# A hybrid layer's read-out in four groups of four tiles, and an output projection that turns x1 itself

## The chip, the cores and the metric

The kernel runs on one core of one Trainium2 chip. The metric is device time in microseconds (us), the median of several executions. Lower is better. All data is float32. A float32 product on TensorE is recorded as two matmul instructions, so "x2" in a row is one product.

## What is computed

One layer with a context prefix (256 tokens) and a latent stream (512 tokens), 1024 channels. What the change touches, cut from the reference:

```python
# per direction d of the recurrence: y is (tokens, heads, 64)
outs.append(group_norm(y, lnx_w, lnx_b) + bonus)          # mean and variance over the 64 of a head
rwkv_y = (outs[0] + outs[1]) * g                          # g = sigmoid(xg) @ g2
pool_y = (box_mean(u) - u) @ pool_w * pool_scale           # four windows: 2, 4, 8, 16
m = (sigmoid(gl_p) * (pool_y @ pool_proj) + sigmoid(gl_r) * (rwkv_y @ rwkv_proj)) @ w_out
h = x + gt1 * rmsnorm(m, norm_gains[1])                    # x1 below
u = rmsnorm(h, norm_gains[2]) * (1 + sc2) + sh2            # f below
logits = u @ [router_group_w, router_expert_w] + bias      # 36 columns
f = hier_moe(u, ...)                                       # top-1 of 4 groups, top-2 of 8 experts, 32 experts in all
out = h + gt2 * rmsnorm(f, norm_gains[3])
```

## The kernel before

The program is a row of blocks, one after another, each with its own instruction list for every engine and a barrier at its end: `begin`, `low_rank_inputs`, `prepare`, `recurrence` (until 836 us), `read_out`, `merge`, `project_out`, `route`, `experts`. The order in each list is written out by hand, and every cross-engine dependence is a wait for a semaphore. An engine runs its list in order, so a wait holds all that is behind it.

**read_out** (L997). The two directions' outputs are 16 tiles of 128 channels (two heads) x 512 tokens, `tile(d, k)`. For every tile TensorE makes the mean over a head (`ro_mean`, a product with a block matrix, L1060), VectorE subtracts it (L1112), ScalarE squares (L1091), TensorE makes the variance (`ro_var`, L1066), and ScalarE makes 1/root of it as `Ln` (L1099) and `Exp` with a scale of -0.5 (L1102), for two tiles at a time. The root is a full 128 x 512 tile: all 64 rows of a head hold the same numbers. VectorE multiplies (L1117), and for each k adds the two directions (L1122), applies gain and bias (L1124), adds `bonus` (L1126) and multiplies by the gate (L1129), which TensorE made at L1073. Between these lie eight pool steps (L1044 and L1048), alternately four products with a box matrix and one product with `pool_w`, through one PSUM bank that ScalarE reads (L1081, L1083). `y0`, the first direction, comes back from HBM by a transfer issued at the start (L1026). The tiles alternate between `ro_y` (direction 0) and `pool_space` (direction 1).

**merge** (L1138) is 224 products of 128 x 512 on TensorE, with the conditioning rows 2 to 5 of `mod_rows` worked out by VectorE beside them.

**project_out** (L1254). For each of four tiles of 128 tokens, `product` (16 products into `po_ps`, L1306); ScalarE's sum of squares (L1336) and root (L1339), VectorE's normalisation (L1367) and x1 = x + ... (L1369); sum of squares and root of x1 (L1341, L1344), VectorE's scale and shift to f (L1375, L1377), two 128 x 1024 steps; then TensorE turns f (`turn`, L1314), ScalarE copies it (`po_fT`, L1348), and `route` makes the 36 logits (L1322, L1323). TensorE's order is product(0), product(1), turn(0), route(0), product(2), turn(1), route(1), and so on. SyncE's queue loads rows, gains, x and the weights of three experts, then stores x1 and f of each tile, and the block ends when the stores of f have landed.

**route** (L1397) is a chain of small VectorE steps that sorts tokens to experts. SyncE loads the weights of three more experts meanwhile (L1437). It ends in gathers of token rows from f in HBM.

**experts** (L1607). 16 pairs of experts. Per pair: a gather of 128 rows, `turn` (L1644), `copy_xT` on ScalarE (L1653), gate and up products with 32-column tiles (L1794), sigmoid (L1656), two VectorE products (L1662, L1664), a turn, a copy, the down products (L1809), a copy of the result (L1659), a store. Weights live in seven slots. The transfer for expert n of 7 and up waits until the pair that last used its slot is through `down` (L1712). Each expert is 3 MB.

## Time and profile before

| | us |
|---|---|
| runs | 1563.69, 1564.85 (median), 1569.78 |
| profiled execution, its own time | 1565.51 |
| span of the profile | 1563.5 |
| mean granted TensorE clock | 0.939 of 2.4 GHz |
| busy: TensorE, VectorE, ScalarE | 1338.7 (86%), 634.8 (41%), 561.8 (36%) |
| read_out | 836 to 940 |
| merge | 940 to 1154 |
| project_out | 1154 to 1238.5 |
| route, to the first turn of experts | 1238.5 to 1270 |
| experts and the combination | 1270 to 1563.5 |

The time of an execution is 2 us above its span. Busy shares are means over stages that have different limits, so the table is only a map. What each stage waits for has to be read in the stage.

### The profile page before, as it was taken

The numbers are of one execution on the slowest core, as the hardware profiler recorded it, in microseconds if no ns is written. First come the engines' busy times: TensorE is split into PE (matmuls) and PEld (weight loads), VectorE is DVE, ScalarE is ACT, GpSimd is POOL, SyncE is SP. The second block draws the span as 40 slices with busy tenths as digits, with TensorE's granted clock in tenths as the row PEclk, the third lists the DMA queues.
The fourth block names the chain that finished last, engine by engine and source line by source line (L and its number), as shares of the span: only waits on it lengthen the run. The fifth ranks groups of instructions, "written<-read, shape, count | busy, mean of one in ns | idle before, by whom it ended". The sixth has DMA issues, their size and how long they took to land. (4 is left out here: it accounts for less than half of the span.)

```text
span 1563.5 us, 37612 instructions
## 1 busy us (share of the span) xinstructions
PE 1338.7 (86%) x16458; PEld 804.1 (51%) x16458; DVE 634.8 (41%) x982; ACT 561.8 (36%) x859; POOL 234.9 (15%) x191
## 2 busy tenths in 40 slices
PE   5889999999999999999997669899999559777780
PEld 2445555555888888888884224344434323222220
DVE  1357777773455544455442350533413330000004
ACT  4244454542655655565552560000002101111113
POOL 0011123112122433333310000000000011010002
PEclk9999999999999999999998889999999669998995
DMA  8205665546221222222205009644446369999985
GB/s 369 88 1 160 176 186 151 168 117 190 101 71 71 71 77 78 77 78 78 78 11 231 5 0 369 255 147 156 155 169 266 156 259 399 423 427 424 424 351 188
DMA packets 102761, 281.42 MB, mean 180 GB/s; under 512 B 18627, under 2 KB 67907, under 8 KB 88531
## 3 DMA queue, kind: packets, MB, share of 16 engines
q1 hardware_dynamic: 96660, 249.81, 43.0%
q0 software_dynamic: 5952, 29.36, 4.8%
q8 instruction: 126, 2.06, 0.5%
q14 instruction: 23, 0.19, 0.0%
HBM read 234.05 MB, written 53.49 MB: 184 GB/s over the span
## 5 line engine op out<-in xcount | busy, mean ns | idle before, releaser
L391 PE MATMUL pr_ps<-hT,pr_w 128*128 128x512 f32 x384 | 172.2, 602 | 4.0 <-DVEq L99 4.0
L972 DVE COPY_PREDICATED rc_T<-masks_sb,rc_ps 128x512 f32<-128x512 uint32 x96 | 65.2, 729 | 151.3 <-PE rc_ps L761 151.3
L391 PEld LDWEIGHTS pr_ps<-hT,pr_w 128*128 128x128 f32 x384 | 72.1, 191 | 94.9 <-issue 90.1
L1200 PE MATMUL mg_ps<-hT,mg_w 128*128 128x512 f32 x256 | 113.6, 602 | 3.2 <-PEq L1021 3.2
L1662 DVE TENSOR_TENSOR mg_w<-mg_w,ex_pgu 128x256 f32<-128x256 f32 x16 | 6.7, 422 | 192.4 <-ACT mg_w L1656 192.4
L1200 PEld LDWEIGHTS mg_ps<-hT,mg_w 128*128 128x128 f32 x256 | 49.5, 194 | 66.8 <-issue 66.8
L761 PE MATMUL rc_ps<-rc_T,rc_Z 64*64 64x64 f32 x3840 | 74.1, 221 | 6.8 <-issue 5.3
L1219 ACT ACTIVATE mg_sig<-mg_ps 128x512 f32<-128x512 f32 x16 | 9.6, 597 | 188.5 <-PE mg_ps L1200 188.5
L912 ACT ACTIVATE rc_G<-rc_ps 128x512 f32<-128x512 f32 x120 | 66.4, 599 | 24.0 <-PE rc_ps L761 23.3
L734 PE MATMUL rc_ps<-masks_sb,rc_T 128*128 128x128 f32 x480 | 67.6, 281 | 5.1 <-DVE rc_Tf L970 4.7
L761 PEld LDWEIGHTS rc_ps<-rc_T,rc_Z 64*64 64x64 f32 x3840 | 64.7, 134 | 13.3 <-issue 8.0
L501 POOL TENSOR_TENSOR pr_kd<-pr_rate,pool_space 128x768 f32<-128x768 f32 x16 | 29.0, 1812 | 279.5 <-DVE pr_kraw L543 279.5
L936 POOL TENSOR_TENSOR rc_Z<-rc_Z,masks_sb 64x512 f32<-64x512 f32 x48 | 64.4, 1341 | 42.6 <-ACT rc_Z L894 40.0
L914 ACT ACTIVATE rc_Tt<-rc_ps 128x512 f32<-128x512 f32 x120 | 66.8, 609 | 5.6 <-PE rc_ps L734 5.5
L894 ACT ACTIVATE rc_Z<-rc_ps 128x1024 f32<-128x1024 f32 (+1 forms) x48 | 41.5, 881 | 75.5 <-PE rc_ps L727 75.5
L1656 ACT ACTIVATE mg_w<-ex_pgu 128x256 f32<-128x256 f32 x16 | 6.1, 384 | 160.5 <-PE ex_pgu L1794 160.5
L761 PE MATMUL rc_ps<-rc_G,rc_Tt 64*64 64x64 f32 x3072 | 56.9, 221 | 3.9 <-issue 2.2
L1306 PE MATMUL po_ps<-pl_w_box,merged 128*128 128x512 f32 x128 | 57.3, 608 | 2.8 <-PEq L1155 2.8
L399 PE MATMUL pr_ps<-hT,pr_w 128*128 128x256 f32 x256 | 57.9, 379 | 0.0
L1200 PE MATMUL mg_ps<-rwkv_y,mg_w 128*128 128x512 f32 x128 | 57.6, 603 | 0.0
L734 PEld LDWEIGHTS rc_ps<-masks_sb,rc_T 128*128 128x128 f32 x480 | 51.2, 141 | 11.4 <-DVE rc_Tf L970 6.5
L761 PEld LDWEIGHTS rc_ps<-rc_G,rc_Tt 64*64 64x64 f32 x3072 | 50.3, 134 | 10.7 <-issue 5.3
(352 smaller groups left out, 2608.4 us busy)
## 6 DMA issues: line engine op xcount, KB each, us to landing
bonus_sb<-in_ada_w SPq DMA_DIRECT2D x16, 1024.0 KB, 7.0
mg_w<-in_w_merge SPq DMA_DIRECT2D x8, 1792.0 KB, 7.4
pr_w<-in_w_prep SPq DMA_DIRECT2D x8, 1664.0 KB, 9.7
kr_chunks<-pr_KR SPq DMA_DIRECT2D x16, 768.0 KB, 4.2
bk_chunks<-pr_BK SPq DMA_DIRECT2D x16, 768.0 KB, 6.5
rc_BK<-bk_chunks SPq DMA_DIRECT2D x24, 512.0 KB, 4.2
rc_KR<-kr_chunks SPq DMA_DIRECT2D x24, 512.0 KB, 4.3
rwkv_y<-in_w_experts SPq DMA_DIRECT2D x5, 2048.0 KB, 17.7
```

What stands on the lines that cost most here:

```text
L391: last = pe.matmul(lat_bank[:, :], wv[:, j * KT + kt, :], hT[:, kt, lat], start=(kt == 0), stop=(kt == KT - 1))
L399: last = pe.matmul(ctx_bank[:, 0:CTX], wv[:, j * KT + kt, :], hT[:, kt, 0:CTX], start=(kt == 0), stop=(kt == KT - 1))
L501: pool.tensor_tensor(kd[:, d, :], rate[:, d, :], k_ka[:, :], ALU.mult)
L734: last = pe.transpose(out[:, q // Q, q % Q * P:q % Q * P + P], src(q), g["ident"])
L761: last = pe.matmul(out[to, k, q * C:q * C + C], lhs(at, q, s, b), rhs(at, q, s, b), start=True, stop=True)
L894: act.activation(Z[u][:, d // 2, :, at:at + Q, 0:w], src.rearrange("p b (j n) -> p b j n", n=P)[:, :, :, 0:w], ACT.Copy).then_inc(act_s, 1)
L912: act.activation(G[:, d, :, :, :], src[:, :, 0:Q * C].rearrange("p s (q t) -> p s q t", q=Q), ACT.Copy).then_inc(act_s, 1)
L914: act.activation(Tt[:, d, :, :, :], turned, ACT.Copy).then_inc(act_s, 1)
L936: pool.tensor_tensor(first, first, both[OWN[side], 0:C].unsqueeze(1).unsqueeze(1).to_broadcast([HD, 2, Q, C]), ALU.mult)
L972: dve.copy_predicated(T[u][:, d, :, :, :].rearrange("p q b t -> p b q t"), level(int(s[1:]), d), by_side).then_inc(dve_s, 1)
L1200: last = pe.matmul(ps[u][j][:, :], w[:, u, w0 + k, :], rhs, start=(k == 0), stop=(k == n - 1))
L1306: last = pe.matmul(ps[t % 2][:, h * 512:h * 512 + 512], merged[:, k, t * P:t * P + P], w[:, k, h * 512:h * 512 + 512], start=(k == 0), sto ...
```

## The change

In `read_out` the 16 tiles are taken in four groups of four, ordered (direction 1, k), (0, k), (1, k+1), (0, k+1). The four variances of a group are products with 32 columns of the block matrix, each into its own 32 rows of one PSUM bank. `Ln` and `Exp` then run once on that bank. A new matrix `spread` brings 32 rows back to 128 by a product over 32 rows for each tile (L1083 of the changed kernel, `ro_root`), and VectorE multiplies from PSUM. Twice the bias is added to `bonus` by ScalarE at the start, and gain and bonus become one VectorE step. The box products skip columns that are zero, the pool has two PSUM banks, and its steps are in another order.

In `project_out` x1 itself is turned and copied, in halves. The gain of the norm goes into the router's weights (`rw_scaled`), the shift into a bias made once by nine products (L1386, L1387), and the root is applied by VectorE when it reads the logits. What is stored for the gathers is x1 times its root (`normed`, ScalarE). `copy_xT` in `experts` applies scale and shift, in eight steps instead of one. Scale and shift come as columns, by two transfers whose runs are one element of 4 bytes long (`f_cols`, 1024 elements each). The block no longer waits for the stores of f: the fifth expert's load and the gathers do.

```diff
-        sq, rs = later[:, 0:2 * SEQ].rearrange("p (v n) -> p v n", v=2), later[:, 2 * SEQ:6 * SEQ].rearrange("p (v n) -> p v n", v=4)
+        sq, rs = later[:, 0:4 * SEQ].rearrange("p (q n) -> p q n", q=4), later[:, 4 * SEQ:6 * SEQ].rearrange("p (v n) -> p v n", v=2)
+        spread, odd = later[:, 6 * SEQ:6 * SEQ + P], sb("ro_odd", [P, 1])
+        ROWS = [slice(32 * q, 32 * q + 32) for q in range(4)]
+        GROUPS = [[(1, 2 * i), (0, 2 * i), (1, 2 * i + 1), (0, 2 * i + 1)] for i in range(KT // 2)]
+        NGR = len(GROUPS)
         diff = merged[:, 0:4, :]
         gates = ctx.enter_context(nc.psum_tensor("ro_gates", [P, SEQ], F32))
         means = [ctx.enter_context(nc.psum_tensor(f"ro_mean{k}", [P, SEQ], F32)) for k in range(2)]
-        varis = [ctx.enter_context(nc.psum_tensor(f"ro_var{k}", [P, SEQ], F32)) for k in range(4)]
-        pooled = ctx.enter_context(nc.psum_tensor("ro_pool", [P, SEQ], F32))
+        varis = ctx.enter_context(nc.psum_tensor("ro_var", [P, SEQ], F32))
+        roots = [ctx.enter_context(nc.psum_tensor(f"ro_root{k}", [P, SEQ], F32)) for k in range(2)]
...
-                            last = pe.matmul(pooled[:, :], g["u"][:, t, j * P:j * P + P], pb["box"][:, j, t, :], start=(t == 0), stop=(t == NT - 1))
+                            a, b = spans[j][t]
+                            last = pe.matmul(pooled[n % 2][:, a:b], g["u"][:, t, j * P:j * P + P], pb["box"][:, j, t, a:b], start=(t == 0), stop=(t == NT - 1))
...
+                def variances(i):
+                    pe.wait_ge(sq_s, 4 * i + 4)
+                    if i:
+                        pe.wait_ge(rs_s, i)
+                    for q in range(4):
+                        last = pe.matmul(varis[ROWS[q], :], g["mean_w"][:, 48:80], sq[:, q, :], start=True, stop=True)
+                    last.then_inc(var_s, 1)
+                def spread_roots(i, half):
+                    pe.wait_ge(rs_s, i + 1)
+                    if 2 * i + half:
+                        pe.wait_ge(yn_s, 2 * (2 * i + half))
+                    for v in range(2):
+                        q = 2 * half + v
+                        last = pe.matmul(roots[v][:, :], spread[ROWS[q], :], rs[ROWS[q], i % 2, :], start=True, stop=True)
+                    last.then_inc(root_s, 1)
+                    k = 2 * i + half
+                    if k == 0:
+                        pe.wait_ge(loaded, 16)
+                    else:
+                        pe.wait_ge(gated, k)
+                    pe.matmul(gates[:, :], g2[:, k * P:k * P + P], g["xg"][:, :], start=True, stop=True).then_inc(gate, 1)
+                mean(0, 0)
                 pool_step(0)
...
+                for q in range(1, 4):
+                    mean(0, q)
+                variances(0)
+                pool_step(1)
+                for i, first, second in ((1, (2,), ()), (2, (3, 4), ()), (3, (5,), (6,)), (4, (7,), ())):
+                    if i < NGR:
+                        for q in range(4):
+                            mean(i, q)
+                    spread_roots(i - 1, 0)
+                    if i < NGR:
+                        variances(i)
+                    for n in first:
+                        pool_step(n)
+                    spread_roots(i - 1, 1)
...
+                act.activation(b2[:, :], chan[:, 33:41], ACT.Copy, scale=2.0)
+                act.drain()
+                for k in range(KT):
+                    act.activation(g["bonus"][:, k, :], g["bonus"][:, k, :], ACT.Identity, bias=b2[:, k:k + 1])
+                for i, reads in ((0, (1,)), (1, (2,)), (2, (3, 4)), (3, (5, 6))):
+                    if i:
+                        act.wait_ge(var_s, i)
+                    for q, (d, k) in enumerate(GROUPS[i]):
+                        act.wait_ge(cen_s, 4 * i + q + 1)
+                        act.activation(by_chunk(sq[:, q, :]), tile(d, k), ACT.Square).then_inc(sq_s, 1)
+                        if i + q == 0:
+                            read_pool(0)
+                    act.wait_ge(var_s, i + 1)
+                    if i >= 2:
+                        act.wait_ge(root_s, 2 * (i - 1))
+                    act.activation(rs[:, i % 2, :], varis[:, :], ACT.Ln, bias=g["gn_eps"])
+                    act.drain()
+                    act.activation(rs[:, i % 2, :], rs[:, i % 2, :], ACT.Exp, scale=-0.5).then_inc(rs_s, 1)
+                    for n in reads:
+                        read_pool(n)
+                read_pool(7)
...
+                def finish(i, half):
+                    dve.wait_ge(root_s, 2 * i + half + 1)
+                    for v in range(2):
+                        d, k = GROUPS[i][2 * half + v]
+                        dve.tensor_tensor(tile(d, k), tile(d, k), by_chunk(roots[v][:, :]), ALU.mult).then_inc(yn_s, 1)
+                    out = ry[:, k, :]
+                    dve.drain()
+                    dve.tensor_tensor(by_chunk(out), tile(0, k), tile(1, k), ALU.add)
+                    dve.drain()
+                    dve.scalar_tensor_tensor(out=out, in0=out, scalar=chan[:, 25 + k:26 + k], in1=g["bonus"][:, k, :], op0=ALU.mult, op1=ALU.add)
+                    dve.wait_ge(gate, k + 1)
+                    dve.drain()
+                    dve.tensor_tensor(out, out, gates[:, :], ALU.mult).then_inc(gated, 1)
+                centre(0)
+                for i in range(1, NGR + 1):
+                    if i < NGR:
+                        centre(i)
+                    for half in range(2):
+                        finish(i - 1, half)
...
+                with nc.allow_non_contiguous_dma(reason="two rows of 4 KB turned into columns"):
+                    sp.dma_start(fcols[:, 0, :], column(2)).then_inc(loaded, 16)
+                    sp.dma_start(fcols[:, 1, :], column(1)).then_inc(loaded, 16)
...
+                def turn(t):
                     for h in range(2):
-                        for k in range(KT):
-                            last = pe.matmul(ps[t % 2][:, h * 512:h * 512 + 512], merged[:, k, t * P:t * P + P], w[:, k, h * 512:h * 512 + 512], start=(k == 0), stop=(k == KT - 1))
-                    last.then_inc(pe_m, 1)
-                def turn(t):
-                    pe.wait_ge(dve_f, t + 1)
-                    if t:
-                        pe.wait_ge(act_fT, t)
+                        pe.wait_ge(dve_x, 2 * t + h + 1)
+                        if t:
+                            pe.wait_ge(act_xT, 2 * t + h - 1)
+                        for k in range(HK * h, HK * h + HK):
+                            last = pe.transpose(pt[:, k, :], x1[:, t, k * P:k * P + P], g["ident"])
+                        last.then_inc(pe_t, 1)
+                def route(t):
+                    if t >= 1:
+                        pe.wait_ge(dve_l, t)
...
+                        if k % HK == 0:
+                            pe.wait_ge(act_xT, 2 * t + k // HK + 1)
+                        last = pe.matmul(pl[t % 2][:, 0:36], xT[:, t % 2, k, :], rw_scaled[:, k, :], start=(k == 0), stop=(k == KT - 1))
+                    last.then_inc(pe_l, 1)
+                for h in range(2):
+                    product(0, h)
+                pe.wait_ge(dve_r, 1)
+                for k in range(KT):
+                    pe.matmul(pl[1][:, 0:36], shift[:, k, :], rw[:, k, :], start=(k == 0), stop=False)
+                pe.matmul(pl[1][:, 0:36], g["mask"]("ones")[0:1, :], rb[:, :], start=False, stop=True).then_inc(pe_l, 1)
                 for t in range(NT):
                     if t + 1 < NT:
-                        product(t + 1)
+                        product(t + 1, 0)
                     turn(t)
+                    if t + 1 < NT:
+                        product(t + 1, 1)
                     route(t)
...
+                def mean_square(t, x, at):
+                    act.activation(sq, x, ACT.Square, accum_out=st[:, t, at:at + 1])
+                    act.drain()
+                    act.activation(st[:, t, at + 1:at + 2], st[:, t, at:at + 1], ACT.Sqrt, scale=1.0 / D, bias=g["small"][:, 1:2]).then_inc(act_root, 1)
+                def copy(t, h):
+                    act.wait_ge(pe_t, 2 * t + h + 1)
+                    if t >= 2 and h == 0:
+                        act.wait_ge(pe_l, t)
+                    act.activation(xT[:, t % 2, HK * h:HK * h + HK, :], pt[:, HK * h:HK * h + HK, :], ACT.Copy).then_inc(act_xT, 1)
...
+                    mean_square(t, ps[t % 2][:, :], 0)
+                    copy(t, 0)
+                    act.wait_ge(dve_x, 2 * t + 2)
+                    mean_square(t, x1[:, t, :], 4)
+                    copy(t, 1)
+                    act.wait_ge(dve_r, t + 2)
                     if t >= 2:
-                        act.wait_ge(pe_l, t - 1)
-                    act.activation(fT[:, t % 2, :, :], pt[:, :, :], ACT.Copy).then_inc(act_fT, 1)
+                        act.wait_ge(g["f_stored"][t % 2], 16 * (t // 2))
+                    act.activation(normed[:, t % 2, :], x1[:, t, :], ACT.Copy, scale=st[:, t, 7:8]).then_inc(act_n, 1)
...
+                dve.wait_ge(loaded, 96)
+                dve.tensor_tensor(row, row, gain, ALU.mult)
+                dve.scalar_tensor_tensor(out=fcols[:, 0, :], in0=fcols[:, 0, :], scalar=1.0, in1=g["chan"][:, 45:53], op0=ALU.add, op1=ALU.mult)
+                dve.tensor_copy(shift, fcols[:, 1, :].unsqueeze(2).to_broadcast([P, KT, P]))
+                dve.drain()
+                dve.tensor_tensor(rw_scaled[:, :, :], rw[:, :, :], fcols[:, 0, :].unsqueeze(2).to_broadcast([P, KT, 36]), ALU.mult)
+                dve.drain().then_inc(dve_r, 1)
+                dve.wait_ge(pe_l, 1)
+                dve.tensor_copy(bias[:, :], pl[1][:, 0:36]).then_inc(dve_l, 1)
...
+                    for h in range(2):
+                        dve.scalar_tensor_tensor(out=ft[:, half(h)], in0=ps[t % 2][:, half(h)], scalar=st[:, t, 3:4], in1=row[:, half(h)], op0=ALU.mult, op1=ALU.mult)
                     dve.drain()
...
+                    for h in range(2):
+                        dve.tensor_tensor(x1[:, t, half(h)], x1[:, t, half(h)], ft[:, half(h)], ALU.add).then_inc(dve_x, 1)
...
+                    dve.reciprocal(st[:, t, 7:8], st[:, t, 5:6])
+                    dve.drain().then_inc(dve_r, 1)
+                    dve.wait_ge(pe_l, t + 2)
+                    dve.scalar_tensor_tensor(out=logits[:, t, :], in0=pl[t % 2][:, 0:36], scalar=st[:, t, 7:8], in1=bias[:, :], op0=ALU.mult, op1=ALU.add).then_inc(dve_l, 1)
...
                 for u in range(EARLY, FIXED):
+                    if u == BESIDE_ROWS:
+                        for v in range(2):
+                            sp.wait_ge(g["f_stored"][v], NT // 2 * 16)
...
         def copy_xT(act, v):
-            return act.activation(xT[:, v, :, :], p_x[:, :, :], ACT.Copy)
+            for k in range(KT):
+                last = act.activation(xT[:, v, k, :], p_x[:, k, :], ACT.Identity, scale=fcols[:, 0, k:k + 1], bias=fcols[:, 1, k:k + 1])
+            return last
```

Three places in the order of the instructions. ScalarE in `read_out`, before: one round of two tiles (`mg_w` holds squares and roots).

```order

```


And now, the second group of four tiles:

```order

```


Two table loads now stand for four tiles, with one `Ln` and one `Exp` of half the size.

TensorE in `read_out`, before (two rounds):

```order

```


And now, from the second group's means to the third's:

```order

```


The means of the next group stand ahead of the roots of this one, and the variances and a pool step stand between its two halves.

TensorE in `project_out`, before, from the start:

```order

```


And now:

```order

```


The turn has moved into the middle of the next tile's product, the logits behind it, and the row of nine bias products stands behind the first product.

## Rows read from the trace of the kernel before

**Rows 1.** Windows by stage: length, each engine's busy time (instructions), PEclk, DMA share, GB/s
```profile
836.00:940.00 104.00, 67.01 (x121) 26.30 (x121) 41.95 (x65) 52.70 (x65) 0.00 (x0) 0.81 0.22 86
940.00:1154.00 214.00, 205.62 (x465) 86.93 (x465) 66.46 (x96) 10.79 (x17) 2.23 (x4) 0.98 0.53 198
1154.00:1238.50 84.50, 72.83 (x232) 39.45 (x232) 25.29 (x35) 15.73 (x29) 0.00 (x0) 0.90 0.54 219
1360.00:1400.00 40.00, 33.57 (x264) 11.51 (x257) 2.54 (x6) 5.18 (x7) 3.07 (x4) 0.90 1.02 426
```

**Rows 2.** Waits of SyncE's queue in experts: us, times, longest
```profile
SPq L1712 <- PE ex_py L1809: 179.4, 13, 17.4
```

**Rows 3.** Timeline of SyncE's queue: the first load after a down product
```profile
1290.06 0.34 SPq L1603 DMA_DIRECT2D rwkv_y<-in_w_experts  x1
```

**Rows 4.** Groups of ScalarE in read_out: xcount, busy, mean ns, idle before
```profile
L1099 ACT ACT_TABLE_LOAD x8 | 10.3, 1283 | 0.1
L1099 ACT ACTIVATE mg_w<-ro_var,small_sb 128x512 f32<-128x512 f32 x16 | 10.1, 684 | 0.1
L1102 ACT ACTIVATE mg_w<-mg_w 128x1024 f32<-128x1024 f32 x8 | 8.5, 1056 | 0.1
```

**Rows 5.** Waits in read_out: us, times, longest
```profile
DVE pool_space L1112 <- PE ro_mean L1060: 38.5, 7, 8.5
```

**Rows 6.** Timeline of one round of read_out: start, length, idle before
```profile
873.01 1.28 ACT L1102 ACT_TABLE_LOAD   x1
874.30 1.06 ACT L1102 ACTIVATE mg_w<-mg_w 128x1024 f32<-128x1024 f32 x1
875.99 5.40 PE L1044 MATMUL ro_pool<-pl_w_box,pool_space 128*128 128x512 f32 x8 [3.75 <-ACT pool_y L1083]
```

**Rows 7.** Groups of VectorE in read_out
```profile
L1117 DVE TENSOR_TENSOR ro_y<-ro_y,mg_w 128x512 f32<-128x512 f32 x8 | 5.5, 688 | 3.1 <-ACT mg_w L1102 3.1
```

**Rows 8.** Timeline of TensorE at the start of read_out
```profile
847.63 1.12 PE L1060 MATMUL ro_mean<-ro_y,mean_w 128*128 128x512 f32 x2 [0.49 <-DMA ro_y<-y_chunks]
```

**Rows 9.** Timeline of VectorE at the start of project_out
```profile
1164.66 1.23 DVE L1353 TENSOR_TENSOR bonus_sb<-bonus_sb,po_gains 128x1024 f32<-128x1024 f32 x1 [12.40 <-DMA po_gains<-in_gains]
```

**Rows 10.** Timeline of TensorE in experts: 32-column products, then a full one
```profile
1282.18 0.59 PE L1794 MATMUL ex_pgu<-rwkv_y,hT 128*32 128x512 f32 x2
1282.19 0.59 PE L1794 MATMUL ex_pgu<-mg_w,hT 128*32 128x512 f32 x2
1282.61 0.60 PE L1794 MATMUL ex_pgu<-rwkv_y,hT 128*32 128x512 f32 x2
1283.14 0.55 PE L1644 MATMUL ex_px<-masks_sb,hT 128*128 128x128 f32 x3
```

**Rows 11.** Timeline of TensorE in the recurrence: 64 x 64 tiles
```profile
801.10 1.16 PE L761 MATMUL rc_ps<-rc_G,rc_Tt 64*64 64x64 f32 x64
```

**Rows 12.** Timeline of the end of project_out
```profile
1219.64 1.04 PE L1314 MATMUL po_pt<-masks_sb,hT 128*128 128x128 f32 x8
1221.79 1.98 PE L1322 MATMUL po_pl<-po_rw,po_fT 128*128 128x36 f32 x16 [1.11 <-ACT po_fT L1348]
1237.96 0.31 DVE L1379 COPY logits<-po_pl 128x144 f32<-128x144 f32 x1 [7.37 <-PE po_pl L1323]
```

**Rows 13.** Groups of project_out
```profile
L1367 DVE SCALAR_TENSOR_TENSOR hT<-po_ps,po_st,bonus_sb 128x1024 f32<-128x1024 f32 x4 | 5.1, 1284 | 0.4
L1341 ACT ACTIVATE bonus_sb<-hT 128x1024 f32<-128x1024 f32 x4 | 4.2, 1056 | 11.7 <-DVE hT L1369 11.7
```

**Rows 14.** DMA share in 40 slices of 326 to 340 us, and packets
```profile
DMA  9999999999999991000000000000000000000000
DMA packets 2981, 1.51 MB, mean 108 GB/s; under 512 B 32, under 2 KB 2981, under 8 KB 2981
```

**Rows 15.** ScalarE: a step with scale and bias columns; the first copy_xT
```profile
L166 ACT ACTIVATE hT<-hT,mod_cols 128x256 f32<-128x256 f32 x8 | 4.0, 588 | 1.4 <-DVEq L196 1.4
1272.14 1.02 ACT L1653 ACTIVATE hT<-ex_px 128x1024 f32<-128x1024 f32 x1 [24.94 <-PE ex_px L1644]
```

211 lines of the change are left out of this document (70 added, 141 removed).

## The prediction

> **What bounds the kernel now.** I read the windows by stage first, then the waits and the timeline of each stage that the diff touches. The profiled execution took 1565.51 us by its own time, 2.0 above its span and 0.7 above the median of the runs, 1564.85. The sum below is made against 1565.5. About 0.5% (8 us) is what a measurement of this kernel can tell from no change.
>
> merge is TensorE's: busy 205.6 of 214 us [rows 1]. The change leaves it alone, so it moves as a whole. From 1290 us on, experts is bound by transfers: DMA share 1.02 at 426 GB/s in a window of 40 us [rows 1], while SyncE's queue waits 179 us for down products, which free the weight slots [rows 2]. The first such load goes out at 1290.06 [rows 3]. So whatever lets the first down product end earlier moves the end of the kernel one to one, and TensorE or ScalarE work inside the later pairs costs nothing while it stays under the transfers.
>
> read_out is bound by no engine: of 104 us VectorE is busy 42, ScalarE 53, TensorE 67, at a granted clock of 0.81 [rows 1]. What it shows is a ring. VectorE waits 38.5 us for means in 7 waits of up to 8.5 us [rows 5]. The means stand in TensorE's list behind a pool step, and that waited 3.75 us for ScalarE's read [rows 6], which stood behind two table loads, two `Ln` and an `Exp`. The loads alone are 8 x 1.28 for `Ln` and as many for `Exp` [rows 4, 6].
>
> **read_out after the change.** ScalarE loses 8 of 16 loads (8 x 1.28 = 10.3 us), 12 of 16 `Ln` (12 x 0.6 = 7) and 8 x 1.06 of `Exp` against 4 x 0.63 (6) [rows 4]. It gains 8 additions of the bias of about 0.6, which run before 847.6 us, when the first direction lands [rows 8] and ScalarE has nothing to do. VectorE loses one step of eight k, about 4 us of its 42. TensorE loses a quarter of the 16 box products' columns, and 12 variance products' time where the four of a group run side by side.
>
> The gain is not these sums but the ring that opens: the means of the next group stand ahead of this group's roots. I walk VectorE's list with 0.69 a step [rows 7] and 0.61 where steps follow without a drain. A finish of one k (two products with roots, sum, gain with bonus, gate) is 3.6. Four centres are 3.6 too, since each mean needs 0.86 (two passes of 0.43 [rows 10]) and alternates with them. y lands at 847.6; group 0's centres, squares, variance, two loads, `Ln` and `Exp` take until 857.3. Meanwhile TensorE does box 1 (2.4), so group 1's centres end at 860.3. Two finishes: 868.0. Then centres 3.6 and finish 3.8; the second half waits 3.3 behind variance, product and box 2 in TensorE's list; finish 3.6: 882.2. The third group the same with box 3, a wait of 2.8: 896.0. Two last finishes: 903.0. That is at 2.4 GHz throughout. Bookkeeping of this sort for the list of before, with TensorE's steps stretched by 1/0.81, ends at 935 where the trace has 940, so I add 3 for what it misses, and 2 for stretches at 1.2 GHz. **908, that is 32 us saved.** At full speed TensorE's 60 products of before are 60 x 0.86 = 52 us in 104, at the clock of 0.81 [rows 1]; now 52 products' worth, 45 us, stand in 67, with shorter gaps between them. That speaks for a higher clock.
>
> The unknowns are the products on parts of the array. Trace of before: products with 32 columns each, four instructions per 0.43 us [rows 10], and 64 products of 64 x 64 in 1.16 us [rows 11]. So the four variances should run side by side, 0.86 for a group. Products over 32 rows into all 128 columns are not in the trace. Their ends are 0.86 for a pair (side by side) and 1.7 (one after another); I take 0.86, by the row of 64 x 64 tiles, which is the nearest. One after another the stage ends 6 later. From 32-column to full products the trace shows a start 0.53 after the last, 0.10 above the usual 0.43 [rows 10]; each TensorE step carries 0.1 in my walk. The Trainium skill (TensorEngine Tiling (Array Packing), Key Properties) says that a change of tiling mode drains TensorE, and the new list changes it some 24 times; the page gives no time. If a drain were the whole latency of a product, 0.17 beyond its pass, the sum would rise by under 2. Bounds for the stage: 903 (saves 37), and 924 with the clock at 0.81 and roots one after another (saves 16).
>
> The Trainium skill (ScalarE: Activation LUTs, What ACT_TABLE_LOAD costs) puts a switch at 1.28 for the load and 1.38 for a drain. Rows 6 show the load at 873.01 and `Exp` at 874.30, so the trace has 1.28 alone. By the page's price the loads taken out would be worth 21 instead of 10 in ScalarE's list.
>
> **project_out.** Of 84.5 us, before: four products of 13.7, and per tile a turn, a wait of 1.1 for the copy, and logits of 2.0 with 0.4 for the bias [rows 12]. The last product ends at 1219.6 where turn(2) starts, and the logits are read at 1238.0 [rows 12]: a tail of 18.9 to the stage's end. After, up to the last product's end: two waits for the copy go (2.2), since logits come half a product later, and two bias products (0.8). Nine bias products come (2.4), turn(2) moves ahead (1.0), and there is a wait of about 1.5 for `dve_r`: the rows that VectorE needs land near 1165 as now [rows 9], and four VectorE steps (3.1) follow, against 1167.7 for the end of product(0) (1153.9, where merge ends, and 13.8). That is 1.9 more; with fewer waits I take 1.6 off for stretches at the lower clock (0.90 in the stage [rows 1]), so the last product ends at 1219.9. Behind it: sum of squares 1.06 and root 0.5; VectorE 2 x 1.4 in halves instead of 1.28 + 1.23 [rows 13], 4.9 in all to x1; then the store of x1, issued and landed in 6. The f steps (1.28 + 1.23) and the wait for them are gone, as is ScalarE's copy ahead of the sum (1.0), and turn, root, copies and logits (5.2) lie beside the store. I get 11.5 to the end, 7.4 less than 18.9. **7 saved**, between 3 (columns late, clock low in the tail) and 10.
>
> The columns: 2 x 1024 runs of 4 bytes. 2981 packets of 512 bytes kept all 16 transfer engines busy for 15 slices of 0.35 = 5.3 us [rows 14], 28 ns each and engine. 2048 more packets are 128 per engine, 3.6 us, while 1.5 MB of rows less (3.6 us at 426 GB/s [rows 1]) go. So I set them against each other. In SyncE's queue x and three experts' weights stand behind them. If x comes 3 us later, so does the first x1, but turn(0) stands behind nine bias products and half a product (2.4 + 6.9), which cover it; the weights are first read in experts. Behind the moved wait for f's stores stand only experts 5 and 6, wanted by the third pair.
>
> **route** keeps its 24 us chain. **The first pair** pays for eight steps in `copy_xT`: 128 x 256 with two columns took 0.588, with eight in 4.0 [rows 15]. For 128 columns I take 0.39 each, 3.1 in all against 1.02 [rows 15]: **2 lost**, between 1 and 3. In later pairs it lies beside the down products (3.4) and under the transfers.
>
> Sum: 1565.5 - 32 - 7 + 2 = **1528.5, told as 1528**.
>
> **Rivals.**
> 1. *The ring opens, TensorE stays slow.* The clock stays at 0.81 as before, roots run one after another: stage at 924, project_out saves 5. 1565.5 - 16 - 5 + 2 = 1546. For it: idle gaps remain around each group. Against: the gaps are shorter.
> 2. *The copy takes the place.* If pair after pair waited for `copy_xT`, 15 x 2.1 = 32 would come back: 1559. Against: in TensorE's list a turn and the down products (4 x 0.86 + 0.4 = 3.8) lie between a pair's turn and its gate products, more than 3.1, and transfers bound the stage. It decides once the copy passes 3.8 us and the lateness of every pair the transfers' lead.
> 3. *Slower: small products at half speed.* If 32-column and 32-row products run one after another and the stage falls to 1.2 GHz throughout, each step in VectorE's ring waits for TensorE: my walk ends at 983, 43 later than now. 1565.5 + 43 - 7 + 2 = 1603. It turns to a loss once the stage ends past 945. Against: [rows 10, 11].
> 4. *The columns stall.* If one 4-byte run took 0.3 us and engine, 128 would take 38, and gain would be gone. Against: [rows 14]. I count it with case 2 as no change.
>
> **Chances.** The forecast 0.72, case 1 0.2, cases 2 and 4 0.05, case 3 0.03. The forecast's own range is 1518 (37 + 10 - 1 saved) to 1540; with case 1 in it, the range is 1517 to 1547. Faster 0.92, same 0.05, slower 0.03.
>
> **What would show it.** read_out 68 to 76 us long, 8 table loads in it, TensorE's clock 0.9 or more, VectorE waiting 3 us at each second half; four `ro_var` products in under 1.1 us; `ro_root` pairs 0.9 apart; project_out 76 to 78 long with no wait of TensorE between products but the one for `dve_r`; eight steps in the first `copy_xT` in about 3.1; merge 214; the DMA share in experts 1.0 from the first down product on. I would be wrong if merge grew, if experts lengthened, or if `ro_root` took 1.7 a pair and the means waited for it.

## The result, and the profile after the change

The change runs in 1523.35 us (median of 4, 1522.52 to 1524.61), the kernel before beside it in 1564.27 (1562.38 to 1569.78): a ratio of 0.9733, 95% interval 0.9715 to 0.9751, or 41 us saved where 37 were forecast. By the spans of the two profiled executions it is 1563.5 - 1521.0, 42.4 us before rounding. I cut both at the same instructions, from where SyncE issues the first load of read_out to where TensorE starts merge, and so on:

| stage, us | before | after | difference | forecast |
|---|---|---|---|---|
| ahead of read_out (same code) | 836.5 | 834.5 | -1.9 | 0 |
| read_out | 103.5 | 69.2 | -34.3 | -32 |
| merge | 213.9 | 213.5 | -0.4 | 0 |
| project_out | 84.6 | 77.2 | -7.4 | -7 |
| route, to the first turn of experts | 31.6 | 31.7 | +0.1 | 0 |
| first turn to the first load behind a down product | 19.9 | 21.3 | +1.4 | +2 |
| rest | 273.4 | 273.7 | +0.3 | 0 |

The first line is no gain of the change: ahead of read_out, the executions profiled here took between 833.9 and 844.3 us, whatever the kernel. For small effects the stages are the finer measure, but a stage too can differ between two executions of one kernel by the clock that TensorE is granted: read_out of the change is 69.2 here, and 70.4 in each of the two later profiles of it.

The windows by stage of the change, which answer to [rows 1] (length, busy time of TensorE, weight loads, VectorE, ScalarE and GpSimd with instructions, granted clock, DMA share, GB/s):

```profile
834.50:903.60 69.10, 54.23 (x152) 19.36 (x153) 38.24 (x59) 35.34 (x50) 0.00 (x0) 0.93 0.33 129
903.60:1117.20 213.60, 205.43 (x465) 86.74 (x465) 66.47 (x96) 10.82 (x17) 2.23 (x4) 0.97 0.52 198
1117.20:1194.40 77.20, 73.95 (x242) 40.57 (x242) 15.42 (x33) 20.73 (x38) 0.00 (x0) 0.92 0.56 217
1320.00:1360.00 40.00, 33.18 (x268) 11.60 (x262) 3.37 (x8) 10.61 (x26) 3.07 (x4) 0.91 1.02 427
```

In read_out VectorE still has 38.2 us of work (42 before), now in 69 us instead of 104; ScalarE fell from 52.7 to 35.3 and TensorE from 67.0 to 54.2, at a clock of 0.93 instead of 0.81 (0.88 in the two later profiles). ScalarE is busy twice as long in a window of experts (10.6 of 40), and the DMA share there is 1.02 as before.

VectorE's waits in read_out, which answer to [rows 5]:

```profile
DVE ro_y L1158 <- PE ro_mean L1066: 12.2, 6, 10.5
DVE pool_space L1164 <- PE ro_root L1083: 8.2, 6, 3.5
DVE pool_space L1158 <- PE ro_mean L1066: 8.1, 6, 5.1
```

The waits for means of `pool_space` fall from 38.5 us to 8.1, and 5.1 of these are one wait ahead of the second group's means. The other large ones left are 10.5 for y of the first direction to land, and the waits for roots. A round in the timeline (start, length, idle before):

```profile
872.13 1.07 PE L1074 MATMUL ro_var<-mg_w,mean_w 128*32 128x512 f32 x8
873.13 1.12 PE L1056 MATMUL ro_pool<-merged,pl_pw 128*128 128x512 f32 x2
874.09 3.17 PE L1052 MATMUL ro_pool<-pl_w_box,pool_space 128*128 128x512 f32 x8
877.19 1.13 PE L1083 MATMUL ro_root<-mg_w 32*128 32x512 f32 x4
878.25 1.12 PE L1090 MATMUL ro_gates<-xg_sb,ro_g 128*128 128x512 f32 x2
...
878.37 0.69 DVE L1164 TENSOR_TENSOR pool_space<-pool_space,ro_root 128x512 f32<-128x512 f32 x1 [3.52 <-PE ro_root L1083]
...
892.50 0.69 DVE L1164 TENSOR_TENSOR pool_space<-pool_space,ro_root 128x512 f32<-128x512 f32 x1 [3.08 <-PE ro_root L1083]
```

Eight instructions are four variances, in 1.07: side by side. Four instructions are the two products that spread the roots, in 1.13: also side by side. Behind the variances stand a pool product and a box step (873.13 to 877.19), and VectorE waits 3.52 and 3.08 for the roots behind them. The walk of the prediction has 3.3 and 2.8 at these two places.

ScalarE's groups in read_out, beside [rows 4]:

```profile
L1137 ACT ACT_TABLE_LOAD x4 | 5.1, 1283 | 0.1
L1139 ACT ACT_TABLE_LOAD x4 | 5.1, 1283 | 0.2
...
L1137 ACT ACTIVATE mg_w<-ro_var,small_sb 128x512 f32<-128x512 f32 x4 | 2.7, 687 | 1.5 <-PE ro_var L1074 1.5
...
L1139 ACT ACTIVATE mg_w<-mg_w 128x512 f32<-128x512 f32 x4 | 2.5, 630 | 0.0
```

Eight loads of 1.28, four `Ln`, four `Exp`, as counted. TensorE's timeline in project_out, and VectorE's first step there:

```profile
1117.15 17.04 PE L1359 MATMUL po_ps<-pl_w_box,merged 128*128 128x512 f32 x32 [2.84 <-PEq L1205]
1134.03 1.87 PE L1386 MATMUL po_pl<-po_rw,bonus_sb 128*128 128x36 f32 x16
...
1183.67 1.87 PE L1378 MATMUL po_pl<-po_rws,po_xT 128*128 128x36 f32 x16
1188.21 1.97 PE L1369 MATMUL po_pt<-masks_sb,hT 128*128 128x128 f32 x8 [2.67 <-DVE hT L1441]
...
1123.99 1.23 DVE L1424 TENSOR_TENSOR bonus_sb<-bonus_sb 128x1024 f32<-128x1024 f32 x1 [8.52 <-DMA f_cols<-mod_rows_dram]
```

The last product ends at 1183.7, 10.7 before the stage does. TensorE doesn't wait for `dve_r`: what VectorE needs is there at 1124, seven us into the stage, where before it was eleven [rows 9]. But product(0) takes 17.04 instead of 13.8: TensorE starts it at half clock, granted 0.50 in its first 5 us where the kernel before has 1.00 (both rows stand with the experiments).

In experts, the first copy of a pair and the first load behind a down product:

```profile
1228.05 2.90 ACT L1727 ACTIVATE hT<-ex_px,f_cols 128x128 f32<-128x128 f32 x8 [24.99 <-PE ex_px L1717]
...
1247.37 0.34 SPq L1676 DMA_DIRECT2D rwkv_y<-in_w_experts  x1
```

### The profile page after: what moved, and what is told of

The parts are those of the page before. It is cut to its first block and busy times, and to the rows that moved or that the text cites. A ratio compares the mean times of both kernels' runs of the same rounds, so it can differ in the third digit from the quotient of the medians.

```text
span 1521.0 us, 37771 instructions
## 1 busy us (share of the span) xinstructions
PE 1328.0 (87%) x16500; PEld 797.3 (52%) x16500; DVE 620.2 (41%) x974; ACT 578.9 (38%) x964; POOL 235.3 (15%) x191
## 5 line engine op out<-in xcount | busy, mean ns | idle before, releaser
L1250 PEld LDWEIGHTS mg_ps<-hT,mg_w 128*128 128x128 f32 x256 | 49.1, 192 | 65.4 <-issue 65.4
L1727 ACT ACTIVATE hT<-ex_px,f_cols 128x128 f32<-128x128 f32 x128 | 46.5, 469 | 34.2 <-PE ex_px L1717 34.2
L734 PEld LDWEIGHTS rc_ps<-masks_sb,rc_T 128*128 128x128 f32 x480 | 51.2, 141 | 11.0 <-DVE rc_Tf L970 6.4
```

The source lines that it names most:

```text
L734: last = pe.transpose(out[:, q // Q, q % Q * P:q % Q * P + P], src(q), g["ident"])
L1250: last = pe.matmul(ps[u][j][:, :], w[:, u, w0 + k, :], rhs, start=(k == 0), stop=(k == n - 1))
L1727: last = act.activation(xT[:, v, k, :], p_x[:, k, :], ACT.Identity, scale=fcols[:, 0, k:k + 1], bias=fcols[:, 1, k:k + 1])
```

## The experiments

The stage lengths below come from each kernel's own profile, cut as in the table above. "To the last gate" is the stretch in read_out from the start of the mean for which y had to land to the start of VectorE's last multiplication by a gate; it leaves out the load ahead of it. In the change's three profiles it is 57.0, 58.2 and 58.2. The difference lies wholly ahead of the first four variances: from the landing of y to them it takes 5.8, 6.9 and 6.9, at a granted clock of 0.70, 0.59 and 0.60. From the first variances to the last gate it is 51.2 in all three, at 1.00. This stretch is the finest measure of a change inside read_out, and is given below as "from the first variances".

**The parts of the change alone.** The kernel before with the new `read_out`, and the change with the old one.

```diff
-def read_out(nc, ...):     # the whole function is exchanged for that of the other kernel
...
+def read_out(nc, ...):
...
```

> The kernel before with read_out of the change alone. Theory (the stages add up, TensorE-bound merge and transfer-bound experts pass a shift on whole): read_out 69 us instead of 103.5, project_out 84.6 and the first copy_xT as before, so 34 to 35 us less than before, about 1529. Rival (part of the gain is made elsewhere, or read_out profits from what else was changed): under 30 us less.

> The change with read_out of before. Theory: project_out 77 us (7.4 less), first pair 1.4 longer, together 6 less than before, about 1558. The two parts alone then give 34.5 + 6 = 40.5 of the 41 to 42 measured. Rival (interaction): the parts do not add up by 3 us or more. The slow first 3 us of product(0) seen in the change (clock 0.50) come again by the theory that they follow from the stage's own start; they are missing if they were chance.

Measured beside a kernel before of 1572.55 us: the new read_out alone 1538.40, ratio 0.979 (0.9764 to 0.9816), 34.1 us; all but read_out 1561.37, ratio 0.9933 (0.9911 to 0.9954), 11.2 us. Together that is 45.3 where the change saved 41, and 4.3 is more than the 3 that the expectation allowed for parts that add. The intervals are wide, 29 to 37 and 7 to 14 us, so the times don't decide it. The stages do. Read_out is 70.0 with the new list and 103.3 with the old one, whatever stands behind it. In both of these profiles TensorE was granted 0.66 in the first 5 us of project_out; the old stage then took 86.3 and the new one 75.9, 10.4 less. In the pair of profiles at the top, the kernel before (first row) had 1.00 there and the change 0.50:

```profile
1153.90:1158.90 5.00, 4.97 (x12) 2.37 (x13) 0.00 (x0) 0.00 (x0) 0.00 (x0) 1.00 0.72 246
...
1117.20:1122.20 5.00, 5.00 (x6) 2.10 (x7) 0.00 (x0) 0.00 (x0) 0.00 (x0) 0.50 0.76 230
```

So the second part is worth more than the pair at the top shows. A low clock at the start is not the new stage's own doing either: here the old stage has it too, though neither has the 0.50.

**No roots spread by products.** Groups of four stay, but each variance is a full 128 x 128 product into its own half of one of two `ro_var` tiles of 1024 columns, `Ln` and `Exp` run over all of it, and VectorE multiplies by the result itself. One pool bank is left instead of two, and one `rs` buffer, so `Ln` waits for VectorE.

```diff
-  pe.matmul(varis[ROWS[q], :], g["mean_w"][:, 48:80], sq[:, q, :], ...)
+  pe.matmul(varis[q // 2][:, q % 2 * SEQ:(q % 2 + 1) * SEQ], g["mean_w"], sq[:, q, :], ...)
-  pe.matmul(roots[v][:, :], spread[ROWS[q], :], rs[ROWS[q], i % 2, :], ...)
```

> The change, with the roots made as before: four products of 128 columns into four banks, two Ln of 1024 and one Exp of 2048 elements a group, no product that spreads them, one pool bank as before. The order of the groups, the means ahead of the roots, the shortened boxes and the two table loads a group stay. Theory (the order and the fewer rounds open the ring, the 32-row products are the smaller part): read_out 74 to 78 us, 5 to 9 more than the change. Rival (the small variances, Ln and Exp are the gain): read_out 90 or more, over 20 us above the change.

Measured: 1545.39 us, ratio 0.984 (0.9814 to 0.9867), read_out 83.3, which is 14.1 more than the change and 20.2 less than before. From the first variances it is 64.2, 12.9 more than the change. That lies between the two expectations. ScalarE's groups and its longest wait:

```profile
L1130 ACT ACTIVATE ro_rs<-ro_var,small_sb 128x1024 f32<-128x1024 f32 x8 | 8.5, 1110 | 4.4 <-PE ro_var L1073 4.4
L1132 ACT ACTIVATE ro_rs<-ro_rs 128x2048 f32<-128x2048 f32 x4 | 7.6, 1909 | 0.0
...
ACT L1130 <- DVE ro_y L1150: 10.0, 3, 4.2
```

16.1 us of `Ln` and `Exp` instead of 5.2, and 10.0 of waits for the single buffer. Nearly 60% of read_out's gain comes without spreading, but this kernel also takes a buffer away, so the 14.1 is an upper bound for what the 32-row form itself gives; how much less it is wasn't tested.

**More table loads.** Between `Ln` and `Exp` of each group, two activations of one column that force one more load each.

```diff
+  act.activation(odd2[:, 0:1], g["gn_eps"], ACT.Exp)
+  act.activation(odd2[:, 1:2], g["gn_eps"], ACT.Ln)
   act.activation(rs[:, i % 2, :], rs[:, i % 2, :], ACT.Exp, scale=-0.5).then_inc(rs_s, 1)
```

> The change with two more table loads and two one-column activations in each group, between Ln and Exp: 4 x (2 x 1.28 + 2 x 0.3) = 12.6 us more in ScalarE's list, eight loads as in the list of before with sixteen in all. Theory (ScalarE has 3 to 8 us to spare between Exp and the product that reads it): 0 to 3 us more. Rival (table loads in ScalarE's list were what read_out paid for): 10 to 13 us more.

Measured: 1529.91 us, ratio 0.9737 (0.971 to 0.9764), read_out 69.9. ScalarE is busy 46.6 instead of 35.3, and read_out is 0.7 us longer than in the first profile of the change and shorter than in the other two; from the first variances it takes 51.6, 0.4 more. In the new list a table load costs next to nothing, even right on the way from variance to root. Its timeline:

```profile
896.27 1.28 ACT L1140 ACT_TABLE_LOAD   x1
897.57 0.20 ACT L1140 ACTIVATE ro_odd<-small_sb 128x1 f32<-128x1 f32 x1
897.77 1.28 ACT L1141 ACT_TABLE_LOAD   x1
899.07 0.20 ACT L1141 ACTIVATE ro_odd<-small_sb 128x1 f32<-128x1 f32 x1
899.28 1.28 ACT L1142 ACT_TABLE_LOAD   x1
```

Three loads with a short step between them follow each other every 1.50. The Trainium skill (ScalarE: Activation LUTs, What ACT_TABLE_LOAD costs) adds a drain of 1.38 to each; these rows leave no room for one.

**The order of the list undone.** Both halves of a group are finished ahead of the means of the next one, on TensorE and on VectorE.

```diff
-  for q in range(4): mean(i, q)
-  spread_roots(i - 1, 0); variances(i); ...; spread_roots(i - 1, 1)
+  spread_roots(i - 1, 0); spread_roots(i - 1, 1)
+  for q in range(4): mean(i, q)
+  variances(i); ...
-  centre(i); finish(i - 1, 0); finish(i - 1, 1)
+  finish(i - 1, 0); finish(i - 1, 1); centre(i)
```

> The change with the order inside read_out undone: both halves of a group are finished before the means of the next group are made, on TensorE and on VectorE; pool steps stand behind the variances. Theory (the gain comes from the ring: the next group's centres fill the time of variance, Ln, Exp and roots): VectorE then idles about 6 us between a group's last centre and its first root three times (4 us less for the first group, and the waits of 3.5 and 3.1 at second halves go), read_out 80 to 88 long instead of 69 to 70, 11 to 18 us slower than the change. Rival (the gain comes from the work taken out: 8 table loads, 12 Ln, 12 variance products; the order is worth little): read_out up by under 5 us.

The change once more, on the same chip, as its partner:

> The change itself once more, unedited, as the partner of the other kernels of this batch. Both theories: a ratio of 0.971 to 0.976 to the kernel before. The profile shows whether TensorE starts project_out at half clock again (0.50 in the first profile of the change, 1.00 in that of the kernel before): if the low clock there belongs to the change, it is there again and product(0) takes 15.5 to 17; if it comes and goes with the execution, it may be 13.8.

Measured beside a kernel before of 1571.97: the change 1531.67, ratio 0.9737 (0.9708 to 0.9766), read_out 70.4, product(0) at 0.51 again. Order undone: 1540.99, ratio 0.9802 (0.9774 to 0.9829), read_out 82.6, 12.2 more; to the last gate 70.3, and from the first variances 64.3, 13.1 more. The theory holds for the stage (80 to 88), and the rival's 5 is far off. VectorE stands still between a group's last centre and its first root:

```profile
DVE pool_space L1163 <- PE ro_root L1083: 26.3, 5, 7.4
```

By the medians it is only 9.3 slower, under the 11 to 18 expected. In its profiled execution TensorE had its full clock at the start of project_out, which makes up 3.0 of such a difference; whether the other executions had it too isn't on record. The profile gives the length of the new stage at full clock:

```profile
1138.18 13.97 PE L1358 MATMUL po_ps<-pl_w_box,merged 128*128 128x512 f32 x32 [2.84 <-PEq L1204]
```

74.2 us, against 84.6 for the old one at the same clock: 10.4 again.

**Pool steps moved.** No box step stands between two halves any more; box steps stand among the means of the next group, or between groups.

```diff
-  pool_step(1)
-  for i, first, second in ((1, (2,), ()), (2, (3, 4), ()), (3, (5,), (6,)), (4, (7,), ())):
+  for i, among, between, second in ((1, (1,), (), (2,)), (2, (), (), (3,)), (3, (4,), (), (5,)), (4, (), (6,), (7,))):
...
```

> The change with no box step between the two halves of a group: box steps stand among the means of the next group, products of the pool behind the second half. Theory (the waits of 3.5 and 3.1 us at the second halves are the pool product and the box step ahead of the second roots in TensorE's list): both waits fall below 1 us, means are late by up to 1 us for a group instead, read_out 64 to 66 instead of 69 to 70, 4 to 6 us faster than the change. Rival (TensorE is the bound of the group: about 11.6 us of products against 11.2 of VectorE's steps, so the wait only moves to the means): read_out stays above 68, under 1.5 us gained.

Measured: 1526.88, ratio 0.972 (0.9688 to 0.9751), 4.8 less than the change beside it (their runs overlap: 1525.8 to 1531.4, and 1529.3 to 1534.8). Read_out is 66.5, 3.9 less than its partner's 70.4, to the last gate 54.2. About 1 of the 3.9 is the clock between y and the first variances (0.72 here, 0.59 in the partner; 6.0 us and 6.9); from the first variances it is 48.2, 3.0 less. VectorE's waits:

```profile
DVE pool_space L1160 <- PE ro_mean L1066: 11.4, 6, 2.9
DVE ro_y L1160 <- PE ro_mean L1066: 11.4, 6, 10.4
DVE pool_space L1166 <- PE ro_root L1083: 3.3, 4, 2.2
```

The waits for roots fall from 8.2 to 3.3, so the box step was what the second half waited for; but one of 2.2 is left where the theory had under 1, and means now wait behind box steps, 2.9 at a time. Just under half of the 6.6 us of the two waits is real gain (3.0), and the rest moves with the box steps.

**The copy of a pair in 32 and in 16 steps,** instead of 8.

```diff
-  act.activation(xT[:, v, k, :], p_x[:, k, :], ACT.Identity, ...)
+  for c in range(0, P, 32):
+      act.activation(xT[:, v, k, c:c + 32], p_x[:, k, c:c + 32], ACT.Identity, ...)
```

(In the second kernel 64 stands for 32.)

> The change with the copy that scales and shifts the tokens of a pair in 32 steps of 32 columns instead of 8 of 128 (about 8 to 9 us instead of 2.9). Theory (transfers bound the pairs; TensorE's list needs gate products 6.9, turn 1.1 and the longer of the copy and 4.5 us of other work, 17.0 us a pair with this copy against 17.1 us by the transfers): the first pair is 5.5 to 6 later, the last pair and the one spilled tile as much again at most, 6 to 18 us slower than the change in all. Rival (the copy takes its price in each pair, case 2 of the prediction): 15 pairs by 5 us, 75 us slower.

Measured: 1582.87, ratio 1.0064 (1.0042 to 1.0086), 51.2 slower than the change. Neither expectation holds: the first pair is 6.3 later, as the theory says, but the rest grows by 45. One pair in the timeline:

```profile
1309.99 1.09 PE L1717 MATMUL ex_px<-masks_sb,hT 128*128 128x128 f32 x8
...
1311.12 8.73 ACT L1728 ACTIVATE hT<-ex_px,f_cols 128x32 f32<-128x32 f32 x32 [0.60 <-PE ex_px L1717]
...
1319.90 1.07 PE L1870 MATMUL ex_pgu<-mg_w,hT 128*32 128x512 f32 x3 [7.93 <-ACT hT L1728]
...
1324.96 0.60 PE L1870 MATMUL ex_pgu<-mg_w,hT 128*32 128x512 f32 x3
...
1329.35 1.09 PE L1717 MATMUL ex_px<-masks_sb,hT 128*128 128x128 f32 x8
```

From turn to turn 19.36 us, above the 17.1 that the transfers need. My 17.0 missed that TensorE, after 7.9 us of waiting, runs the first gate products at half clock (granted 0.50 from 1319.9 to 1323.3; 0.85 from start to start instead of 0.43), so that they take 9.45 instead of 6.9. The wait makes the work behind it dearer. The 15 intervals from turn to turn average 18.9.

It also missed that not every pair of the change takes 17.1. The first weights are there early, and up to the seventh turn the pairs follow each other every 12.0 to 14.4, the second and third turn for instance:

```profile
1240.45 1.09 PE L1717 MATMUL ex_px<-masks_sb,hT 128*128 128x128 f32 x8
...
1253.38 1.09 PE L1717 MATMUL ex_px<-masks_sb,hT 128*128 128x128 f32 x8
```

The 15 intervals of the change average 15.7, so a kernel with 17.0 for every pair loses 1.3 x 15 = 19 us although it never exceeds 17.1. By this estimate the 48 us by which first and last turn move apart (283.9 instead of 235.7) are 19 of lost lead and 29 of lower clock (18.9 against 17.0). The transfers are half idle early on: their share from 1300 to 1340 is 0.55 here (first row) and 1.01 in the change.

```profile
1300.00:1340.00 40.00, 25.10 (x184) 7.58 (x188) 2.54 (x6) 21.51 (x74) 1.53 (x2) 0.81 0.55 218
...
1300.00:1340.00 40.00, 31.47 (x252) 10.35 (x244) 2.54 (x6) 8.62 (x20) 3.07 (x4) 0.87 1.01 426
```

> The change with the scaling copy of a pair in 16 steps of 64 columns (4.5 to 5.2 us instead of 2.9; the 32 steps took 8.7 and made the pair's period 18.4 to 19.4). Theory (a pair's ring on TensorE and ScalarE is the copy plus about 9.9 us: 14.5 to 15.1 here, under the 17.1 of the transfers): only the first pair pays, 1.6 to 2.3 us, and the pairs and the last tile little more; 1.5 to 5 us slower than the change, DMA share in the pairs 1.0. Rival (the copy costs in each pair in proportion, a third of the 51 us that the 32 steps cost): 14 to 20 us slower, DMA share 0.95 or less.

Beside it the change a third time:

> The change once more, unedited, as the partner of the kernels of this batch: ratio 0.971 to 0.976 to the kernel before, read_out 69 to 70.5. Project_out 77 if TensorE starts it at half clock, 74 if at full clock.

Measured beside a kernel before of 1567.17: the change 1528.17, ratio 0.9744 (0.973 to 0.9759), read_out 70.4, project_out 77.2 with a start at 0.50. The 16 steps: 1528.94, ratio 0.975 (0.9735 to 0.9765), 0.8 slower by the medians, 2.4 by the stages from the first turn on. The theory had 1.5 to 5, the rival 14 to 20. A copy takes 4.83; the first pair is 1.8 later (23.1 instead of 21.3), the rest 0.6 longer. Early pairs follow each other every 13.0, where the change has 12.9. The share of the transfers is full:

```profile
1420.00:1460.00 40.00, 28.22 (x216) 9.58 (x220) 2.54 (x6) 13.18 (x38) 3.64 (x5) 0.87 1.01 425
```

So behind the first pair the copy is all but free up to somewhere between 4.8 and 8.7 us, and the change's 2.9 is well below.

**All box products over 512 columns again.**

```diff
-  spans = [[(0, SEQ)] + [... columns that box product t of j reaches ...] for j in range(4)]
+  spans = [[(0, SEQ)] * NT for j in range(4)]
```

> The change with all four products of a box step over 512 columns again (before the change too; the change cuts them to the columns reached). From the change's own trace, box steps 1, 2 and 3 take 2.4, 3.1 and 3.6 us; at 0.43 a pass all would take 3.6. Theory: box 1 stands ahead of the second group's means and box 2 between two halves, so read_out grows by 1.2 and 0.5, 1.7 us in all, time 1 to 2.5 us slower. Rival (a longer busy TensorE is granted its clock sooner, or the steps lie beside other waits): no difference, read_out 69 to 70.5.

Measured: 1528.49, ratio 0.9747 (0.9732 to 0.9762), 0.3 slower; read_out 69.6. Box steps are longer as expected: VectorE waits 6.3 and 3.9 where the change has 5.1 and 3.5, and from the first variances it takes 52.8, 1.6 more. That much of the theory holds. But the rival holds too, and the 1.6 comes back at the start: the first box step, at half clock, now runs until y is there, and TensorE has its full clock from then on.

```profile
843.94 6.47 PE L1052 MATMUL ro_pool<-pl_w_box,pool_space 128*128 128x512 f32 x8 [3.06 <-DMA pl_w_box<-in_pool_box]
850.34 1.12 PE L1066 MATMUL ro_mean<-ro_y,mean_w 128*128 128x512 f32 x2
...
854.82 1.07 PE L1074 MATMUL ro_var<-mg_w,mean_w 128*32 128x512 f32 x8 [1.44 <-ACT mg_w L1131]
```

From y to the first variances it takes 4.5 us here at a granted clock of 1.00. The change, where TensorE has waited 2.4 to 2.6 for y, takes 5.8 in its first profile and 6.9 in the other two. So the shortened boxes were worth nothing on balance in this kernel. That the wait ahead of y is what lowers the clock is argued and not shown: there is one profile without that wait, against eleven with it (clock 0.59 to 0.73).

**Both directions' order too.** The kernel with the pool steps moved, and both tiles of direction 1 first in each group, so that two centres and squares are done before y of direction 0 lands.

```diff
-  GROUPS = [[(1, 2 * i), (0, 2 * i), (1, 2 * i + 1), (0, 2 * i + 1)] for i in range(KT // 2)]
+  GROUPS = [[(1, 2 * i), (1, 2 * i + 1), (0, 2 * i), (0, 2 * i + 1)] for i in range(KT // 2)]
...
```

> The kernel with the pool steps moved, and with both tiles of direction 1 first in each group (the halves then take first and third, second and fourth root), so that two centres and squares instead of one are done before y of direction 0 lands. Theory (VectorE's list sets read_out, and work moved ahead of y's landing shortens it): 1.5 to 2.5 us less than with the pool steps moved alone, read_out 64 to 65.5, 5 to 7 us faster than the change. Rival (the first group's variances and squares hang on y's tiles alone, and the last two centres come no earlier): read_out 66 to 67, as with the pool steps moved.

Measured: 1522.81, ratio 0.9708 (0.9688 to 0.9728), 5.4 less than the change beside it, with the intervals of the two ratios apart. Read_out is 65.4, to the last gate 53.2: about 1 less than with the pool steps moved alone (the theory had 1.5 to 2.5) and 5 less than the change beside it. From the first variances it takes 48.2, as with the pool steps moved alone, so the 1 lies ahead of them, where one centre fewer is left once y has landed (5.0 us instead of 6.0). This is the fastest of the kernels tried. Merge takes 215.5 in it, 2 more than in the change: it lies between 213.2 and 215.8 in the profiles of this study. The wait for `mg_acc` there (5.3 in the change, 8.3 here) doesn't explain it: it is 7.1 in a profile whose merge is 213.3, and 5.8 in one of 215.7. Whether merge gives back a part of what read_out gains wasn't tested.

## Why the prediction was right, and where its terms were off

**read_out: -32 forecast, -34.3 measured.** The ring was the right reading. Undoing the order alone gives back 12.2, making the roots full width again (with one buffer less) 14.1, and doubling the table loads costs 0.7 at most: what counts is what VectorE's list waits for. The walk had 55.4 us from y's landing to the end of the last finish; the trace has 57.7 (845.63 to 903.3). I had added 5 to the walk, of which 2.3 were needed. Up to the end of the first `Exp` both have 9.7, although the low clock right after y lands lies in this stretch (means of 1.64 and 1.91, about 1.3 us in all by the kernel with the long box steps), so the walk was a little long there. The trace then falls behind by 0.9 at the second group: from its first mean to the end of its last centre it takes 4.5, where I had counted 3.6 and left out the mean that VectorE has to wait for first. The other 1.4 are delays of 0.1 to 0.5 at each later step. The two assumptions on products that the trace of before did not show both held at the cheap end: four variances 1.07 (forecast under 1.1), two spreading products side by side, next start 1.06 later (forecast 0.86 and 0.1). One row was misread there: the x64 of [rows 11] are 64 instructions, so 32 products in 1.16, and not 64. It still was the nearest row. The sentence on changes of tiling mode (the Trainium skill, TensorEngine Tiling (Array Packing), Key Properties) changed nothing: from variances to a full product the starts lie 1.00 apart, from roots to a gate product 1.06, between two full products 0.86 to 0.96. A change of mode costs 0.2 at most, some 24 times.

One sentence stands on weaker ground. I counted box products with fewer columns among TensorE's savings. They are worth 1.6 behind the first variances, and on balance nothing, since the kernel with the longer steps had TensorE's full clock when y landed.

**project_out: -7 forecast, -7.4 measured, by luck: two errors cancel.** At the same clock in its first 5 us the stage is 10.4 shorter, in two pairs of profiles (86.3 and 75.9 at 0.66; 84.6 and 74.2 at 1.00). That is just outside the bounds that I gave it, 3 to 10. My sum had the last product's end 0.3 later than before; at full clock it is 2.2 earlier (63.5 us into the stage instead of 65.7). Of these 2.5 us, 1.5 is the wait for `dve_r`, which never came: I had taken the small loads to land near where they did before, and they land early, at 1124, ahead of x and the weights. The other 1.0 is in small terms: the nine bias products take 2.1 instead of 2.4, the two waits for the copy were worth more, and logits take 1.7 a tile instead of 1.9. The tail is 10.7 against 11.5.

The 1.6 that I took off for stretches at low clock held. The old stage has one product of 15.5 instead of 13.8 behind its waits in both of its profiles, and no product behind the first is above 13.9 in the twelve profiles of the new stage. What I had no term for is the first product. It lost 3 us to the clock in the profiled execution, and this hid the 3 us that the sum had missed. The clock at that place was 0.50 or 0.51 in four profiles, 0.66 to 0.71 in eight, and 1.00 in two, one of them the profile of the kernel before.

**The first pair: +2 forecast, +1.4 measured.** The copy takes 2.90 (forecast 3.1), 1.9 more than the single step [rows 15]. In other kernels with the eight steps this stretch is 20.4 to 20.9 long, and in the change itself 21.2 to 21.3. Later pairs don't pay: 273.7 to the end against 273.4.

**merge, route, experts** kept their lengths within 0.4, and the columns' 4-byte packets delayed nobody. SyncE's four issues of x took 4.57 in all, and the weights behind them were needed only in experts.

**The rivals.** Case 1 (TensorE stays slow) fell: clock 0.93 in read_out (0.88 in the later two, under the 0.9 that I had named as a sign), roots side by side. Case 3 (serial small products) fell with the same rows. Case 2 is real as a mechanism but far away: the prediction put its point at a copy of 3.8 us plus the transfers' lead; the runs put it between 4.8 and 8.7. Case 4 did not occur. A slip in the range: 46 us off 1565.5 are 1519.5, not 1518, which changes nothing here.

The total came out 4 us beyond the forecast by the medians, and 5.4 by the profiled pair: 2.3 from read_out, 1.1 from project_out, merge, the first pair and the rest together, and 1.9 from the part that the change doesn't touch.

## What to carry to other kernels

Where several engines hand one buffer round and none is busy over two thirds, look at what stands ahead of the awaited instruction in the other engine's list: here the order of products alone was worth 12 us, and eight more table loads on ScalarE cost 0.7 at most. Cut a saving into stages at the same instructions, and compare a stage only between executions with the same granted clock at its start; a stage's -7.4 was -10.4. Work under a bound is free only up to the bound's period, and only where that bound holds: with transfers at 17.1 a pair but a mean of 15.7, because the first pairs run ahead, 17.0 for every pair is already a loss. Past that point TensorE's waits came with half clock in the products behind them, so the loss grew faster than the overrun.

## What the runs showed of the hardware

- Products of 32 rows into 128 columns run side by side: two of them (four instructions) in 1.13 us, the same as one full product (1.12). The two read different groups of 32 rows and write different banks; other arrangements were not tried.
- Ahead of project_out TensorE is idle for 2.84 us in every profile (2.83 to 2.85), yet it is granted anything from 0.50 to 1.00 in the next 5 us. The change has 0.50 or 0.51 in all three of its profiles and so has the kernel with 32 steps; the one with 16 steps, the same up to there, has 0.68. What decides it stays open.
- In the one profile in which TensorE works right up to the landing of y it has a granted clock of 1.00 behind it; in the eleven in which it has waited 2.4 to 3.1 us it has 0.59 to 0.73.
- Two loads of 1024 runs of 4 bytes each were issued in 0.38 and 0.58 us, and the step that waited for them began 4.2 us after the end of the second issue.
- A ScalarE step from the turned tokens' bank costs 0.36 us with 128 columns, 0.30 with 64 and 0.27 with 32 (2.90, 4.83 and 8.73 us for 8, 16 and 32 steps). A line through these is about 0.24 for each instruction and 1 ns for each column, an estimate from the three.
